# A chain of two transformer blocks on one core: weight tiles split in halves, the setup's stream cut to scale and shift, the gate's products moved into the context pass, the bias table written in four parts

## The reference, cut to what matters

```
sh, sc, g = split(silu(c) @ w_mod[l] + b_mod[l], 3)     # for x (from c) and for ctx (from c_ctx)
h    = x * (1 + sc) + sh                                # 2048 wide
cu, cb, cc, cg, q, k, v, ag, pu, pg = split(h @ w_in[l])
y    = [short conv | differential attention, 8 heads | multi-scale pooling]
x    = layernorm(alpha * x + g * (y @ w_out[l]))
```

## Time and profile before

| what | value |
|---|---|
| median of 3 runs | 3694.35 us (3692.41 to 3698.99) |
| the profiled execution | 3697.44 us, its span 3695.9 us |
| TensorE busy | 93% of the span |
| VectorE busy | 62% |
| ScalarE busy | 35% |
| mean granted TensorE clock | 0.964 |
| first product of the context pass | 180.77 us |

### The profile page before, as it was taken

One profiled execution on the slowest core, in us unless ns is written; L12 is line 12 of the kernel. 1 busy time (PEld: TensorE's weight loads), 2 busy tenths in 40 slices (PEclk: granted clock), 3 DMA queues, 4 the chain that ended last, 5 costly groups with the idle time before them and its releaser, 6 DMA issues.

```text
span 3695.9 us, 48538 instructions
## 1 busy us (share of the span) xinstructions
PE 3438.7 (93%) x16800; PEld 2716.5 (74%) x16800; DVE 2290.7 (62%) x2909; ACT 1303.5 (35%) x1730; POOL 209.9 (6%) x396
## 2 busy tenths in 40 slices
PE   8699998899999999998799999999998988998996
PEld 2299988678767777788688777777875777787784
DVE  5455655787676775656555576765655888544433
ACT  0044543432333433225522344433226212344323
POOL 1000000000000000110000000000110000000000
PEclk9889999999999999998899999999999999999998
DMA  9944445445222222563455232321652222221231
GB/s 359 291 151 177 159 154 213 151 170 197 106 103 100 105 97 72 215 215 138 177 197 180 105 113 107 107 95 72 220 189 91 91 79 91 76 78 63 104 115 65
DMA packets 95164, 516.32 MB, mean 140 GB/s; under 512 B 11536, under 2 KB 11568, under 8 KB 55760
## 3 DMA queue, kind: packets, MB, share of 16 engines
q1 hardware_dynamic: 51328, 343.95, 25.6%
q0 software_dynamic: 43728, 170.91, 13.6%
HBM read 492.80 MB, written 22.02 MB: 139 GB/s over the span
## 4 chain that ended last, share of the span: by engine, by line
PE 64%; DVE 14%; issue 7%; DVEq 6%; DMA 4%; ACT 4%; ACTq 1%; POOL 0%; SPq 0%; POOLq 0%; PEldq 0%
PE acc L990 18%; PE acc L991 18%; PE acc L992 18%; DVE xy L1860 5%; PE pv L1070 2%; DVE w_lo L1367 2%; DVE gates L1414 2%; DVEq L1859 2%; PE S L1051 2%; PE S L1229 2%; DVEq L1403 1%; DMA xy<-in_wm 1%; ACT w_hi L540 1%; PE misc L1211 1%; PE S L1059 1%
## 5 line engine op out<-in xcount | busy, mean ns | idle before, releaser
L990 PE MATMUL acc<-h_hi,w_hi 128*128 128x512 f32 (+1 forms) x4736 | 1757.0, 371 | 146.9 <-DVE h_lo L1373 68.5
L991 PE MATMUL acc<-h_lo,w_hi 128*128 128x512 f32 (+1 forms) x4736 | 1715.3, 362 | 0.0
L992 PE MATMUL acc<-h_hi,w_lo 128*128 128x512 f32 (+1 forms) x4736 | 1714.2, 362 | 0.0
L990 PEld LDWEIGHTS acc<-h_hi,w_hi 128*128 128x128 f32 x4736 | 911.2, 192 | 340.8 <-issue 127.3
L992 PEld LDWEIGHTS acc<-h_hi,w_lo 128*128 128x128 f32 x4736 | 911.3, 192 | 135.8
L991 PEld LDWEIGHTS acc<-h_lo,w_hi 128*128 128x128 f32 x4736 | 912.9, 193 | 130.7 <-issue 6.5
L1367 DVE TENSOR_TENSOR w_lo<-raw,w_hi 128x2048 fp32r<-128x2048 f32 x296 | 677.5, 2290 | 394.9 <-ACT w_hi L540 389.0
L540 ACT ACTIVATE w_hi<-raw 128x2048 fp32r<-128x2048 f32 x296 | 564.8, 1908 | 6.7 <-DVEq L1358 6.2
L540 ACT ACTIVATE ev<-acc 128x512 f32<-128x512 f32 (+1 forms) x210 | 110.8, 532 | 1014.5 <-PE acc L992 980.6
L1414 DVE SCALAR_TENSOR_TENSOR gates<-gates,csil 128x512 f32<-128x512 f32 x568 | 412.2, 750 | 85.2 <-DMA gates<-in_wm 49.7
L540 ACT ACTIVATE work<-S,small 128x768 f32<-128x768 f32 (+1 forms) x160 | 129.0, 812 | 278.3 <-DVE small L1512 278.2
(11 more groups left out here) (202 smaller groups left out, 2146.3 us busy)
## 6 DMA issues: line engine op xcount, KB each, us to landing
raw<-in_w SPq DMA_DIRECT2D x296, 1024.0 KB, 4.8
gates<-in_wm POOLq DMA_DIRECT2D x216, 512.0 KB, 4.6
xy<-in_wm SPq DMA_DIRECT2D x32, 1024.0 KB, 10.6
x_d<-xy POOLq DMA_DIRECT2D x2, 4096.0 KB, 13.9
vtok<-in_wm POOLq DMA_DIRECT2D x8, 512.0 KB, 7.3
qb<-x_d POOLq DMA_DIRECT2D x16, 256.0 KB, 3.3
kb<-x_d POOLq DMA_DIRECT2D x16, 256.0 KB, 4.0
out_y<-xy POOLq DMA_DIRECT2D x4, 1024.0 KB, 4.1
```

The costliest lines, as they stand in the source:

```text
L990: mm(o, w_hi[:, w], h_hi[:, x], start=n == 0, stop=False)
L991: mm(o, w_hi[:, w], h_lo[:, x], start=False, stop=False)
L992: last = mm(o, w_lo[:, w], h_hi[:, x], start=False, stop=n == len(ks) - 1)
```

## The change

Four things are changed.

1. The setup streams only scale and shift. They come from a new array `wm0` in 32 loads of 1 MB with whole rows of 2048 columns, scale first. PE multiplies each by `csil0`, 32 columns of which two hold the vectors, in four matmuls that write partitions 0 to 31, 32 to 63, 64 to 95 and 96 to 127 of one PSUM bank (`mod0_step`). One evacuation and four transposes replace each stage of row evacuations and column matmuls. The first two weight tiles are loaded before the last eight of the stream.
2. The gate's 32 tiles are made by `mod_tiles` on DVE in the context pass: 8 in `cconv`, 16 in `chead`, 8 in `cout`, and `reduce_mod` once after each 8. The loops over `cconv`, `chead` and `cout` are written out for that on DVE, partly on PE and POOL.
3. The bias table stands in `kb`, and POOL writes it in four DMAs of 4 heads (4 partitions) each, one after each two gate tiles of `cconv`. ACT doesn't wait for it any more; DVE waits for all four before the heads.
4. `hi` and `lo` work on half a tile each (128x1024), with semaphores that count halves; PE waits for `w_lo` at the start and at the middle of a tile, and tells ACT at the middle (`half_done`) and at the end.

```diff
+M0_SLOTS = 4
+M0_STEPS = 2 * KT
-MOD_OF = {"mod0": ((0, 1), 32), "aconv": ((2, 3), 0), ...
+MOD_OF = {"cconv": ((0, 1), 32), "chead": ((0, 1), 36), "cout": ((0, 1), 44), "aconv": ((2, 3), 0), ...
...
             def load(j, src):
-                sp.wait_ge(lo_done, shown(lo_done, j - 1))
+                sp.wait_ge(lo_done, shown(lo_done, (j - 1).times(2)))
                 sp.dma_start(raw[:, j.odd * D:(j.odd + 1) * D], src).then_inc(raw_landed[j.odd], 16)
...
+            for e in range(M0_STEPS):
+                if e == M0_STEPS - 8:
+                    for p in range(2):
+                        load(j_at("cconv", 0, p), w0[p:p + 1])
+                s = e % M0_SLOTS
+                if e >= M0_SLOTS:
+                    sp.wait_ge(m0_used, shown(m0_used, e - M0_SLOTS + 1))
+                sp.dma_start(xy[:, s * D:(s + 1) * D], A["wm0"][e:e + 1]).then_inc(m0_landed[s], 16)
...
-            loop(pool, 0, 4, gates0)
...
-            pool.dma_start(bias_d[0:16 * P * 384].rearrange("(h q n) -> h q n", q=P, n=384),
-                           evt[0:16, 0:384].unsqueeze(1).broadcast_to([16, P, 384])).then_inc(bias_st, 16)
+            for g in range(4):
+                mods("cconv", g, range(2), 2)
+                pool.dma_start(bias_d[g * 4 * P * 384:(g + 1) * 4 * P * 384].rearrange("(h q n) -> h q n", q=P, n=384),
+                               kb[4 * g:4 * (g + 1), 0:384].unsqueeze(1).broadcast_to([4, P, 384])).then_inc(bias_st, 16)
             pool.dma_start(rope, A["rope"]).then_inc(rope_land, 16)
...
                 act.wait_ge(raw_landed[j.odd], shown(raw_landed[j.odd], j.half.times(16) + 16))
-                act.wait_ge(tile_done, shown(tile_done, j - 1))
-                f(w_hi[:, j.odd * D:(j.odd + 1) * D], raw[:, j.odd * D:(j.odd + 1) * D]).then_inc(hi_done, 1)
+                for h in range(2):
+                    used = (half_done, tile_done)[h]
+                    act.wait_ge(used, shown(used, j - 1))
+                    s = slice(j.odd * D + h * D // 2, j.odd * D + (h + 1) * D // 2)
+                    f(w_hi[:, s], raw[:, s]).then_inc(hi_done, 1)
...
-            act.wait_ge(bias_st, shown(bias_st, 16))
...
                 for n, k in enumerate(ks):
+                    if (w_k0 + n) % (KT // 2) == 0:
+                        pe.wait_ge(lo_done, shown(lo_done, j.times(2) + (1 + (w_k0 + n) // (KT // 2))))
...
+                    if w_k0 + n == KT // 2 - 1:
+                        last.then_inc(half_done, 1)
...
+            def mod0_step(e, slot):
+                n, k = e // KT, e % KT
+                pe.wait_ge(m0_landed[slot], shown(m0_landed[slot], 16 * (e // M0_SLOTS + 1)))
+                to = mod0_sums[n]
+                for q in range(4):
+                    last = mm(to[32 * q:32 * (q + 1), :], csil0[:, 32 * k:32 * (k + 1)],
+                              xy[:, slot * D + MC * q:slot * D + MC * (q + 1)], start=k == 0, stop=k == KT - 1)
+                last.then_inc(m0_used, 1)
+            def mod0_transposes(n, to, row):
+                pe.wait_ge(m0_row, shown(m0_row, n + 1))
+                for s in range(MOD_COLS):
+                    last = nc.tensor.transpose(to[:, P * s:P * (s + 1)], row[:, P * s:P * (s + 1)], ident[:])
+                last.then_inc(m0_cols, 1)
...
+                        if c == "c":
+                            mod_tiles(phase, 0, ((), (2 * i,), (), (2 * i + 1,))[p])
...
+                        if p == 1 and i % 4 == 0:
+                            mod_columns(*(("cconv", 0) if i == 0 else ("chead", i // 4 - 1)), gate0_ps)
+                        if proj and p == 2:
+                            mod_tiles("chead", i // 4, (2 * (i % 4),))
                         if proj and p == 3:
...
                             nc.vector.tensor_copy(kb[:, 0:T], ev[1][:, 0:T]).then_inc(qk_ready, 1)
+                            mod_tiles("chead", i // 4, (2 * (i % 4) + 1,))
...
                 if c == "c":
+                    dve.wait_ge(bias_st, shown(bias_st, 64))
```

More of the change, by code:

```diff
@@ L282, in mod, with cout_mods @@
             return modc[:, bass.ds(m + (48 * which + 16 * what), 1)]
+        def cout_mods(i, p):
+            return range(3 * i + p, 3 * i + p + 1) if p < 3 and 3 * i + p < MOD_TILES else ()
         def by_set(which):
@@ L443, in body @@
                                        x[:, bass.ds(i * 4 + p, 1), :]).then_inc(xin_land[p % 2], 16)
-                loop(pool, 0, 4, body)
+                if phase == "cout":
+                    for i in range(4):
+                        body(i)
+                else:
+                    loop(pool, 0, 4, body)
             def store(c, dst, count):
@@ L1027, in conv @@
                     loop(pe, 2, N_CONV, body)
+                elif c == "c":
+                    loop(pe, 0, N_CONV, body)
+                    reduce_mod("cconv", 0, gate0_ps)
                 else:
@@ L1152, in heads @@
                     ctx_step(1, norm=False)
-                    loop(pe, 2, N_HEADS, ctx_step)
+                    for i in range(2, N_HEADS):
+                        ctx_step(i)
+                        if i % 4 == 3:
+                            reduce_mod("chead", i // 4, gate0_ps)
                     ctx_step(N_HEADS, proj=False)
@@ L1340, in pw @@
                     j = j_at("pw", i, t)
-                    pe.wait_ge(lo_done, shown(lo_done, j + 1))
                     for s in range(2):
@@ L1363, in lo @@
             def lo(j):
-                dve.wait_ge(hi_done, shown(hi_done, j + 1))
-                s = slice(j.odd * D, (j.odd + 1) * D)
-                tt(w_lo[:, s], raw[:, s], w_hi[:, s].bitcast(F32), ALU.subtract).then_inc(lo_done, 1)
+                for h in range(2):
+                    dve.wait_ge(hi_done, shown(hi_done, j.times(2) + (h + 1)))
+                    s = slice(j.odd * D + h * D // 2, j.odd * D + (h + 1) * D // 2)
+                    tt(w_lo[:, s], raw[:, s], w_hi[:, s].bitcast(F32), ALU.subtract).then_inc(lo_done, 1)
             def modulated(c, T, i):
@@ L1403, in mod_tiles @@
                             dve.drain()
[L1404 to L1407 removed]
+                        if kk == 0:
+                            landed = m.half.times(16) + 16
                             dve.wait_ge(mraw_landed[m.odd], shown(mraw_landed[m.odd], landed))
@@ L1483, in conv @@
                     loop(dve, 2, N_CONV, body)
+                elif c == "c":
+                    for i in range(N_CONV):
+                        body(i)
                 else:
@@ L1679, in project_out @@
                     body(3, last=True)
+                elif c == "c":
+                    for i in range(4):
+                        body(i)
+                        if i == 2:
+                            mod_columns(phase, 0, gate0_ps)
                 else:
```

192 lines of the change are left out of this document (89 added, 103 removed).

## The result

The changed kernel takes 3669.11 us (median of 4 runs, 3667.41 to 3673.59); the kernel before, in the same comparison, 3696.05 us (3692.41 to 3698.99). The ratio is 0.9929, with a 95% interval of 0.9912 to 0.9947: faster by 0.7%. 3669 us was forecast.

A forecast was written before the change was run, and what follows sets the result against it. TensorE, busy 93% of 3695.9 us, was taken as the bound, with waits to win mainly in the setup. Terms -76 + 45 + 4 + 8 - 6 = -25 gave 3672, or 3669 us against the median; range 3614 to 3694.

The forecast's parts named there:

- The stream: Setup: without the gate's loads and the bias wait, the context pass's first product comes at 105 us, a gain of 76.
- assumed overlap of column groups: Setup stream: products on four column groups run side by side; a factor of 1.5 already hides TensorE behind the stream.
- The bias parts, length: `cconv`: each quarter of the bias write, read from 4 partitions, takes as long as the whole, 30 us.
- The bias parts, price: `cconv`: weight loads that meet a bias part stall TensorE, and slower products follow; 45 us lost, bounds 2 and 60.
- The allowance of 10.2 us: `cconv`: the time a weight load may take before TensorE stalls; a load meeting a part takes 21.2 us.
- The first pause: `cconv`: the first bias part meets the modulation, where TensorE goes at half clock anyway, so its stall was taken as 6 us.
- The gate on VectorE: Context pass: VectorE has room; 3 us lost over all heads and 1 in the output stage, bounds 0 and 25.
- The sums: Context pass: four `reduce_mod` of 16 small records each now stand on a full TensorE, 8 us lost.
- The halves: Weight tiles: earlier halves gain 9 us at six places where stages begin, `glu` loses 3; net gain 6 us.
- Short parts: Rival for `cconv`: bias parts take 7 us each and cost about 2 us, not 45; 3626 us, chance 0.20.
- Serial groups: Rival for the setup: TensorE's column groups don't overlap, first product at 127 + 4 us; some 3692 us, chance 0.05.
- the slower case: Rival for `cconv`: a weight load gets no turn until its bias part ends; four parts cost 100 us; 3724 us, chance 0.08.

The follow-up runs named there:

- e7_one_group_b: e1_repeats with the setup stream's four products of a step written to one column group from each sum's second step on; 3631.16 us.
- e3_spread: The changed kernel with each bias part read from every fourth partition and written to every fourth head slot; 3610.70 us.
- e9_source_only: The changed kernel with each bias part read from every fourth partition but written to the contiguous head slots as before; 3612.72 us.
- e1_repeats: The changed kernel with the four bias writes cut along the 128 repeats, each reading all 16 partitions; 3610.47 us.
- e6_few_gate_ops: e1_repeats with VectorE's gate work in the context pass cut to 2 of 32 operations per chunk, loads and waits kept; 3602.26 us.
- e5_gates_first: e1_repeats with the first two gate tiles of `cout` issued ahead of the two token loads on the GpSimd queue; 3608.71 us.
- h1_halves: The kernel before with only the weight tiles in halves (hi, lo and TensorE's waits by half tiles); 3656.96 us.

## Why the prediction came out right, point by point

The total was right to the microsecond, and that was partly luck: two groups of terms were off by nearly 20 us each, with opposite signs.

- **The stream** (first product at 105 us, gain 76): 104.1 us, gain 76.7. Rate 420 GB/s instead of 409. TensorE waits for the DMA, as forecast. The assumed overlap of column groups is shown by e7_one_group_b: without it the first product comes at 123.9 us, where I had worked out 127 for the stream and 4 behind it, 131 in all.
- **The bias parts, length** ("each as long as the whole, 30 us"): 37.1 us. The step "fewer source partitions, lower rate, in proportion 26 GB/s" gave the right 25 GB/s for the wrong reason. It isn't the number of partitions: every fourth one gives 103 GB/s (e3_spread), and the source alone decides (e9_source_only). It is the number of groups of four neighbours. 786 KB at 25 GB/s are 31 us. About 6 us more are there in the whole write before, too (36.6 us for some 30 us of bytes), and stay unexplained.
- **The bias parts, price** (45 us): mis-sized; 57.9 us (`cconv` of the changed kernel less that of e1_repeats). The mechanism was right in each link: `w_lo`, `hi`, the load of `raw`. Three sizes were off. The load: the three later pauses stand behind loads of 24.0, 22.7 and 21.8 us, mean 22.8, where I took the 21.2 us of the earlier trace rows. The allowance of 10.2 us: these loads less their pauses (13.7, 14.6 and 13.7 us) leave 10.3, 8.1 and 8.1 us. The first pause: 10.0 us and not 6. So the pauses sum to 52.0 us where 39 were forecast. And the slower products behind the pauses cost 9 us and not 6 (113.3 less 104.0 us busy). The kernel with short parts keeps 5.6 us of such waits itself, which is why 52.0 and 9 add to more than 57.9.
- **The gate on VectorE** (4 us): mis-sized, 8.2 us by the medians of e6_few_gate_ops and up to 14.3 us by stages. I had charged the heads and the output stage and let `cconv` go free because it fits on average (24 us of work on 47.35 of 93). It was `cconv` that paid most, 8.6 us. In `cout` I had overlooked that moving the gate's loads puts the first behind 4 MB of tokens on GpSimd's queue (about 5 us, e5_gates_first).
- **The sums** (8 us): in `cout` the 16 records stand between two products that start 1.83 us apart, where 0.12 would do, so 1.7 us, and 7 for all four if the others cost the same. The one behind `cconv` waited 2.3 us more for VectorE.
- **The halves** (-6 us): mis-sized, and the worst term. -37 us alone (h1_halves). In the changed kernel the stages from `aconv` on are 25.7 us shorter, and in h1_halves, which has nothing but the halves, 30.8 us. I counted six places at a stage's start, and there is a wait for `w_lo` in 39 places; with the halves there are 22 of them, the longest 4.6 us and not 6.2. `glu` became 3.8 us shorter instead of 3 longer. That VectorE is busy 42.53 of 50 us didn't mean that its fixed cost sets the time: TensorE's waits for `w_lo` there fell from 25.0 to 16.7 us. The term left the clock out: 17 of the 40 us of h1_halves are less busy time at a higher granted clock, in `kv1` for one (0.88 and not 0.86).
- **The rivals.** Short parts were forecast at 3626 us and came, made by experiment, at 3610, since the slow parts cost 58 us more than the short ones and not 43. Serial groups would have been 3669 + 21 = 3690 us by e7_one_group_b; the forecast's own terms (131 for 105 us) make 3695 and not the 3692 that it gives. A load does get its turn during a part: those issued at 154.93 and 197.58 us landed 11 us before their part did, so the slower case did not come. Its remark that the gain is gone from 25 us a part on is a slip: the other terms gain 70 us, so 17.5 us for each of four parts is enough. Measured were 14.5.

In the sum, against the profiled executions (-27.8 us, where -25 was forecast): the setup -0.7 us from the forecast; the four stages of the context pass +74.6 us and not +57 (45 + 4 + 8), so 17.6 too little; all the rest -25.7 and not -6, so 19.7 too little.

## What to carry to other kernels

Before a write out of SBUF is split, ask which source partitions each part reads. Here a part from one group of four neighbouring partitions moved 25 GB/s, and a part from four such groups 103 GB/s, whether it read 4 partitions or 16. So split such a write over its repeats or over every fourth partition, and not into blocks of neighbours. A long transfer costs more than its bytes: of the weight loads issued beside a part of 35 to 38 us, two landed 14 to 23 us late. Beside parts of 10 to 18 us no load took over 11.3 us, near the 8 to 10 us that this pipeline forgives. Handing a tile over in halves pays at places where the consumer waits for the producer, so count the waits in the trace, not the stage starts.

## What the runs showed of the hardware

- Four neighbouring source partitions (4g to 4g+3) give 25 to 26 GB/s, four from different groups 103, with the same quarter of the DMA engines busy (24.5% and 25.2%). In each slow part two weight loads on another queue took 19 to 28 us; beside the short parts they took at most 11.3 us, where the median is 4.9. The parts from every fourth partition landed after 12.1 to 17.9 us, though 786 KB at 103 GB/s are 7.6; what the rest is was not traced.
- Four products of 512 columns (8 records) on four column groups take 1.07 us, on one group 3.62, both at a granted clock of 1.00 (2.4 GHz). At 0.50 (1.2 GHz) the four groups take 1.94 us.
- In the changed kernel the stream's short bursts on TensorE, with waits between them, ran at a mean granted clock of 0.60 to 0.71 from 15 us on; in e7_one_group_b, busy without a break, it was 1.00. It cost nothing here, because a step of 1.94 us still fits between two landings 2.49 us apart.
- The same 16800 TensorE records were busy 3438.7 us in the kernel before and 3421.6 us with the halves, at mean granted clocks of 0.964 and 0.969: fewer waits came with less busy time.
